# Modulation sums of a two-stage transformer kernel: 512 columns wide, and half of the block pairs summed during the Fourier stage

## What is computed

```python
sc = jax.nn.silu(c)
for l in range(DEPTH):                                  # DEPTH = 2
    mod = (sc @ w_mod[l] + b_mod[l])[:, None, :]        # 1024 -> 6144
    sh1, sc1, g1, sh2, sc2, g2 = jnp.split(mod, N_MOD, axis=-1)
    u = modulate(rms_norm(h, norm1_g[l]), sh1, sc1)
    if l % 2 == 0:    # Fourier mixing and neighbourhood attention, then w_out
        y, yc = even_mixer(u, uc, ...)
    else:
        y = pool_mixer(u, ...)
    h = h + g1 * y
    h = h + g2 * sq_relu_mlp(modulate(rms_norm(h, norm2_g[l]), sh2, sc2), w_mlp1[l], w_mlp2[l])
```

## Time and profile before

| | |
|---|---|
| runs (3) | 2247.85 us median, 2245.47 to 2248.17 |
| profiled execution | span 2244.5 us; its whole time is not listed, the median of the runs is 3.35 above |
| mean granted TensorE clock | 0.960 |
| PE busy | 2097.8 us (93%) |
| DVE busy | 972.6 us (43%) |
| POOL busy | 793.6 us (35%) |
| ACT busy | 684.9 us (31%) |
| DMA | 224.25 MB, mean 100 GB/s |

### The profile page before, as it was taken

How to read it: one execution, slowest core, us unless ns; L and a number is a source line. 1 busy time by engine, 2 the same in 40 slices (tenths; PEclk the granted TensorE clock), 3 DMA queues, 4 the chain that set the end, 5 groups by cost and what they waited for, 6 DMA issues and landing times. The chain is left out here.

```text
span 2244.5 us, 25972 instructions
## 1 busy us (share of the span) xinstructions
PE 2097.8 (93%) x10180; PEld 1690.7 (75%) x10180; DVE 972.6 (43%) x1696; ACT 684.9 (31%) x912; POOL 793.6 (35%) x240
## 2 busy tenths in 40 slices
PE   7998998799999979999998979999996998999998
PEld 3876576587878867888886747888885876888886
DVE  1575469677595735233142281014444123312122
ACT  2322352222122233222123373245543233222122
POOL 2322123344444443444444203442321443444444
PEclk9899999799999979999999999999997999999999
DMA  8163004242352232222222102222120222222221
GB/s 344 44 239 80 1 32 173 115 188 112 150 224 111 100 124 75 94 93 95 106 98 81 57 1 93 94 75 76 57 76 19 97 91 76 94 94 99 105 77 38
DMA packets 42773, 224.25 MB, mean 100 GB/s; under 512 B 12736, under 2 KB 13248, under 8 KB 17216
## 3 DMA queue, kind: packets, MB, share of 16 engines
q1 hardware_dynamic: 42688, 223.08, 27.4%
HBM read 218.86 MB, written 2.10 MB: 98 GB/s over the span
## 5 line engine op out<-in xcount | busy, mean ns | idle before, releaser
L815 POOL TENSOR_TENSOR wl<-raw,wh 128x2048 fp32r<-128x2048 f32 (+1 forms) x155 | 710.9, 4587 | 1279.0 <-ACT wh L461 1279.0
L896 PE MATMUL bank<-uh,wh 128*128 128x512 f32 x1480 | 592.4, 400 | 31.4 <-POOL wl L815 7.3
L897 PE MATMUL bank<-ul,wh 128*128 128x512 f32 x1480 | 583.9, 394 | 0.0
L898 PE MATMUL bank<-uh,wl 128*128 128x512 f32 x1480 | 583.6, 394 | 0.0
L461 ACT ACTIVATE wh<-raw 128x2048 fp32r<-128x2048 f32 (+1 forms) x155 | 292.8, 1889 | 601.6 <-PE bank L898 588.7
L896 PEld LDWEIGHTS bank<-uh,wh 128*128 128x128 f32 x1480 | 283.2, 191 | 98.5 <-issue 27.2
L896 PE MATMUL bank<-ah,wh 128*128 128x512 f32 x816 | 322.8, 396 | 6.4 <-DVE al L1720 6.4
L898 PEld LDWEIGHTS bank<-uh,wl 128*128 128x128 f32 x1480 | 282.5, 191 | 60.7
L897 PEld LDWEIGHTS bank<-ul,wh 128*128 128x128 f32 x1480 | 283.2, 191 | 58.9 <-issue 1.0
L898 PE MATMUL bank<-ah,wl 128*128 128x512 f32 x816 | 320.6, 393 | 0.0
L897 PE MATMUL bank<-al,wh 128*128 128x512 f32 x816 | 317.7, 389 | 0.0
(11 more groups left out here) (211 smaller groups left out, 2100.2 us busy)
## 6 DMA issues: line engine op xcount, KB each, us to landing
raw<-in_w SPq DMA_DIRECT2D x64, 1024.0 KB, 6.7
mraw<-in_w_modr SPq DMA_DIRECT2D x40, 1024.0 KB, 4.9
raw<-in_w_gu SPq DMA_DIRECT2D x22, 1024.0 KB, 4.9
raw<-in_w_hg SPq DMA_DIRECT2D x16, 1024.0 KB, 4.9
modf<-in_w_modf SPq DMA_DIRECT2D x8, 1024.0 KB, 17.8
raw<-in_w_in SPq DMA_DIRECT2D x8, 1024.0 KB, 17.8
raw<-in_w_out SPq DMA_DIRECT2D x8, 1024.0 KB, 6.0
raw<-in_w_dn SPq DMA_DIRECT2D x8, 1024.0 KB, 4.9
```

The lines of the kernel that those rows point to most:

```text
L815: pool.tensor_tensor(wl[:, b % 2, 0:nk], raw[:, b % RAW, 0:nk], f32(wh[:, b % 2, 0:nk]), ALU.subtract).then_inc(split_lo, 1)
L896: pe.matmul(out, ah_, bh, start=first, stop=False)
L897: pe.matmul(out, ah_, bl, start=False, stop=False)
L898: return pe.matmul(out, al_, bh, start=False, stop=last)
```

## The change

- A load keeps its 1 MB but has another shape: 512 columns of half of the 1024 rows, [128, 4, 512] instead of [128, 8, 256]. Loads 2p and 2p + 1 are a pair; `mod_sum(2p)` does chunks 0 to 3 and `mod_sum(2p + 1)` chunks 4 to 7 into the same `acc[p % 2]`, 512 wide. A load is four dependent DVE instructions instead of eight. There are 40 loads and 20 pairs.
- `mod_columns(p)` does four one-column matmuls per pair, `mod_store(p)` stores four columns.
- Pair 0 and pair 1 (loads 0 to 3) stay beside the projections: pair 0 where block 0 stood, pair 1 behind the first half of product 2, where block 1 stood. Nothing of it is beside products 3 to 7.
- Pairs 2 to 5 (loads 4 to 11, `MOD_EARLY` = 4 to `MOD_MID` = 12) are summed during the Fourier stage, each pair's columns behind `fourier_out(g)`. Their buffers `mmid0` and `mmid1` alias the upper halves of `uh` and `ul`; the first load waits for the end of product 7. Their columns go to bank 0.
- Pairs 6 and 7 stay in w_out, behind products 9 and 11. In mlp0 the columns stand behind blocks 1, 3 and 5 of each iteration.
- SP loads cs, w4 and tab earlier, once load 3 is summed, and the mask (moved to another address) later, once the last y is done.
- The constant 1/1024 goes; norms of 1024 use 1/128 and a scale in the root.

Core of the diff:

```diff
+MOD_EARLY, MOD_MID = 4, 12
+        mmid0 = at("mmid0", [P, 4, 2 * BC], F32, 24 * KB)
+        mmid1 = at("mmid1", [P, 4, 2 * BC], F32, 40 * KB)
-        mraw = at("mraw", [P, 2, KC, BC], F32, A + 48 * KB)
+        mraw = at("mraw", [P, 2, 4, 2 * BC], F32, A + 48 * KB)
...
+        def mod_bank(p):
+            return bank[0] if MOD_EARLY <= 2 * p < MOD_MID else bank[7]
+        def mod_part(m):
+            if MOD_EARLY <= m < MOD_MID:
+                return (mmid0, mmid1)[m % 2][:]
+            return mraw[:, m % 2]
...
-                sp.dma_start(mraw[:, m % 2], t["w_modr"][count(m, q, per)]).then_inc(mraw_full[m % 2], 16)
+                if m == MOD_EARLY:
+                    wait_block(sp, 7)
+                sp.dma_start(mod_part(m), t["w_modr"][count(m, q, per)]).then_inc(mraw_full[m % 2], 16)
...
-                load_mod(b)
+                if b < MOD_EARLY:
+                    load_mod(b)
...
+            load(9, t["w_out"][1])
+            for m in range(MOD_EARLY, MOD_MID):
+                load_mod(m)
+            sp.wait_ge(y_full, 2 * FG)
+            sp.dma_start(mask[:], t["mask"]).then_inc(tab_in, 16)
+            for b in range(10, 12):
+                load(b, t["w_out"][b - 8])
             sp.wait_ge(smax, len(ITEMS))
-            for m in range(PROJ, MOD0):
+            for m in range(MOD_MID, MOD0):
                 load_mod(m)
...
+            def mod_columns(p, q=0, per=0):
+                if per or p:
+                    pe.wait_ge(mcol_used, p + per // 2 * q if per else p)
+                mod_summed(pe, 2 * p + 1, q, per)
+                for a in range(4):
+                    last = pe.matmul(mod_bank(p)[:, a:a + 1], acc[:, p % 2, P * a:P * a + P], one_col, start=True, stop=True)
                 last.then_inc(mcol_full, 1)
...
-                    if half == 0:
-                        mod_columns(b - 1)
+                    if half == 0 and b == 2:
+                        mod_columns(1)
...
             for g in range(FG):
                 fourier_y(g)
                 fourier_out(g)
+                if g == 0:
+                    pe.wait_ge(bank_free[bank_of(6, 0)], used(6) + 1)
+                mod_columns(MOD_EARLY // 2 + g)
...
             for b in range(8, 12):
-                product(b, uh, ul, after=lambda half: mod_columns(PROJ + 2 * (b - 8) + half))
+                product(b, uh, ul)
+                if b % 2:
+                    mod_columns(MOD_MID // 2 + (b - 8) // 2)
...
-                        if layer == 0 and j < 6:
-                            mod_columns(MOD0 + j, q, 6)
+                        if layer == 0 and j in (1, 3, 5):
+                            mod_columns(MOD0 // 2 + j // 2, q, 6)
...
+                a, part, k0 = acc[:, m // 2 % 2], mod_part(m), 4 * (m % 2)
+                if m % 2 == 0:
+                    dve.tensor_scalar(a, part[:, 0], csil[:, 0, 0:1], None, ALU.mult).then_inc(macc, 1)
+                for k in range(1 - m % 2, 4):
+                    dve.wait_ge(macc, n + k)
+                    dve.scalar_tensor_tensor(a, part[:, k], csil[:, k0 + k, 0:1], a, ALU.mult, ALU.add).then_inc(macc, 1)
...
+            mod_sum(MOD_EARLY)
+            mod_sum(MOD_EARLY + 1)
             for g in range(FG):
+                if g < FG - 1:
+                    mod_sum(MOD_EARLY + 2 * g + 2)
+                    mod_sum(MOD_EARLY + 2 * g + 3)
                 dve.wait_ge(four_hi, g + 1)
                 dve.tensor_tensor(ul[:, g, :], bank[4 + g % 2][:], f32(uh[:, g, :]), ALU.subtract).then_inc(four_lo, 1)
+                mod_store(MOD_EARLY // 2 + g)
...
-            mod_sum(PROJ)
-            mod_sum(PROJ + 1)
+            mod_sum(MOD_MID)
+            mod_sum(MOD_MID + 1)
             for b in range(8, 12):
                 for half in range(2):
                     add_to_h(b, 2 * (b - 8) + half, mod(0, 2, 2 * (b - 8) + half), 0)
+                if b == 8:
+                    mod_sum(MOD_MID + 2)
+                    mod_sum(MOD_MID + 3)
```

More of the change, by code:

```diff
@@ L124, in build_program @@
         diag = at("diag", [P, 4, P], F32, A + 76 * KB)
-        mask = at("mask", [P, 3, 256], F32, A + 88 * KB)
-        acc = at("acc", [P, 2, BC], F32, A + 88 * KB)
+        mask = at("mask", [P, 3, 256], F32, A + 84 * KB)
+        acc = at("acc", [P, 2, 2 * BC], F32, A + 88 * KB)
         ah = at("ah", [P, KC, S], F32R, A)
@@ L231, in build_program @@
         epsq_col = con[:, C_EPSQ:C_EPSQ + 1]
-        PROJ = 8
         def f32(x):
@@ L385, in _ @@
                     sp.dma_start(dfts[:], t["dfts"]).then_inc(dft_in, 16)
-            for b in range(8, 12):
-                if b == 10:
-                    mod_summed(sp, PROJ - 1)
+                    mod_summed(sp, MOD_EARLY - 1)
                     sp.dma_start(cs[:], t["cs"]).then_inc(w4_in, 16)
@@ L941, in norm_sum @@
                 for a in range(n // P):
-                    pe.matmul(sums_[:, a:a + 1], norm_sqs(name)[:, P * a:P * a + P], ones_d[:, 0:1], start=(a == 0), stop=False, skip_group_check=True)
+                    pe.matmul(sums_[:, a:a + 1], norm_sqs(name)[:, P * a:P * a + P], ones_v[:, 0:1], start=(a == 0), stop=False, skip_group_check=True)
                 pe.wait_ge(sq_ready, 8 * i + 8)
                 for a in range(n // P):
-                    last = pe.matmul(sums_[:, a:a + 1], sq[:, 1, P * a:P * a + P], ones_d[:, 0:1], start=False, stop=(a == n // P - 1), skip_group_check=True)
+                    last = pe.matmul(sums_[:, a:a + 1], sq[:, 1, P * a:P * a + P], ones_v[:, 0:1], start=False, stop=(a == n // P - 1), skip_group_check=True)
                 last.then_inc(sum_full, 1)
                 pe.wait_ge(diag_ready, i + 1)
-                pe.matmul(rms[:, 0:n], ones_d, diag[:, 0:n // P, :].rearrange("p a n -> p (a n)"), start=True, stop=True).then_inc(rms_full, 1)
-            def mod_columns(m, q=0, per=0):
-                if per or m:
-                    pe.wait_ge(mcol_used, count(m, q, per))
-                mod_summed(pe, m, q, per)
-                for a in range(2):
-                    last = pe.matmul(bank[7][:, a:a + 1], acc[:, m % 2, P * a:P * a + P], one_col, start=True, stop=True)
+                pe.matmul(rms[:, 0:n], ones_v, diag[:, 0:n // P, :].rearrange("p a n -> p (a n)"), start=True, stop=True).then_inc(rms_full, 1)
+            def mod_columns(p, q=0, per=0):
[4 more added lines that the diff above has]
+                    last = pe.matmul(mod_bank(p)[:, a:a + 1], acc[:, p % 2, P * a:P * a + P], one_col, start=True, stop=True)
                 last.then_inc(mcol_full, 1)
@@ L1012, in _ @@
                 product(b, uh, ul, after=beside(b))
-            mod_columns(PROJ - 1)
             pe.wait_ge(w4_in, 32)
@@ L1380, in mod_sum, with mod_store @@
             def mod_sum(m, q=0, per=0):
[L1382 removed]
+                n, p = (4 * m + 4 * per * q, m // 2 + per // 2 * q) if per else (4 * m, m // 2)
+                a, part, k0 = acc[:, m // 2 % 2], mod_part(m), 4 * (m % 2)
                 dve.wait_ge(mraw_full[m % 2], 16 * (m // 2 + 1) + 8 * per * q if per else 16 * (m // 2 + 1))
[L1384 to L1387 removed]
+                if m % 2 == 0:
+                    if per and m == MOD0:
+                        dve.wait_ge(mcol_full, p)
+                    elif m >= 4:
+                        dve.wait_ge(mcol_full, p - 1)
+                    dve.tensor_scalar(a, part[:, 0], csil[:, 0, 0:1], None, ALU.mult).then_inc(macc, 1)
+                for k in range(1 - m % 2, 4):
                     dve.wait_ge(macc, n + k)
[L1389 to L1393 removed]
+                    dve.scalar_tensor_tensor(a, part[:, k], csil[:, k0 + k, 0:1], a, ALU.mult, ALU.add).then_inc(macc, 1)
+            def mod_store(p, q=0, per=0):
+                dve.wait_ge(mcol_full, p + 1 + per // 2 * q if per else p + 1)
+                c = 16 + 4 * p
                 if per:
                     c = c + 2 * per * q
[L1396 removed]
+                    out, b = modc[:, bass.ds(c, 4)], bmod[:, bass.ds(c, 4)]
                 else:
[L1398 to L1399 removed]
+                    out, b = modc[:, c:c + 4], bmod[:, c:c + 4]
+                dve.tensor_tensor(out, mod_bank(p)[:, 0:4], b, ALU.add).then_inc(mcol_used, 1)
             dve.wait_ge(const_in, 48)
@@ L1434, in _ @@
             mod_sum(2)
+            mod_sum(3)
+            mod_store(1)
             for b in range(2, 8):
                 for half in (-1, 0, 1):
[L1437 to L1438 removed]
                     if (b, half) in HN_AFTER:
                         hn_scale(HN_AFTER[b, half])
[L1441 to L1443 removed]
             for a in range(2):
```

54 lines of the change are left out of this document (16 added, 38 removed).

## The result

The changed kernel takes 2227.4 us (median of 4 runs, 2222.1 to 2229.0) against 2246.8 of the kernel before beside it (4 runs, 2245.5 to 2248.2): a ratio of **0.9907, 95% interval 0.9894 to 0.9921**. Measured again later, it took 2227.8 (ratio 0.9907, 0.9891 to 0.9924). The forecast was 2225.0, so the sum of -22.9 us met a measured -19.4 (difference of the medians) to -20.9 (by the ratio). One microsecond of the forecast came from its base, 2247.85, the median of three runs; with four it is 2246.8.

The account below looks back on a forecast made before the run. PE was taken as the bound, busy 93% of the span, so time is PE time plus its holes. Terms 21.7 - 15.8 - 0.9 + 3.3 - 13.1 - 3.9 - 14.2 = -22.9 from 2247.85 gave 2225.0 us, range 2216 to 2233.

Parts of the forecast that it names:

- Part 1: Block 2: PE stands 18.3 us before pair 1's columns, waiting for late load 3; head sum 1 comes 21.7 us later.
- Part 2: Projections: without sums 4 to 7 on DVE, no kT or qT waits, -15.8 us; two column groups fewer, -0.9.
- this stays: Claim that DVE stays blocked while POOL splits; a narrow first instruction had taken 4.42 us instead of 0.35.
- Part 3: Fourier: four pairs summed there cost +3.3 us for columns; sums ready 1.5 us ahead at the first pair.
- Part 4: w_out: four sums instead of eight, -13.1 us; then the norm before mlp0, with an earlier load of block 12, -3.9.
- Part 5: mlp0: shorter waits for sums and fewer column groups, 369.0 us, so -14.2; bounds -17 and -10.
- the 0.3 us that stood beside the sum: mlp0: a wide DVE operation could hold a POOL split 0.3 us longer, making the forecast sum 0.3 higher.
- The price of a sum: DVE: a load as four dependent 512-wide instructions of 0.77 us takes 3.0 us; bounds 2.8 and 3.96.
- Rival A: Wide instructions save little, 3.96 us per load; parts 1, 5 and 4 grow by 0.9, 4 and 1: 2231 us; chance 0.10.
- B: Projection holes come back through the norm chain; part 2 gives 3 instead of 15.8: 2237.8 us; chance 0.07.
- C: No wait at block 2, load 3 in time gives 20 us more: 2205 us; chance 0.04.
- D: Slower than before: Fourier-stage loads are slow, 4 loads - 27 us; 2269 us at 17.8 us loads; chance 0.05.

Follow-up runs that it names:

- The third experiment: Changed kernel with load 3 issued ahead of vwin, plus no pair in Fourier: two pairs back beside products 3 to 7, two in w_out; 2210.7 us, ratio 0.9837.
- its narrow twin: Load 3 ahead of vwin, no pair in Fourier, each 512-wide sum instruction split into two of 256 columns; 2247.3 us, ratio 1.0003 to the kernel before.
- the narrow kernel: Changed kernel with every 512-wide sum instruction split into two of 256 columns, same places otherwise; 2234.8 us, ratio 0.9956 to the kernel before.
- the slowed loads: Changed kernel with two extra unused 1 MB loads ahead of each of the eight Fourier-stage loads; 2252.6 us, ratio 1.0023 to the kernel before.
- the kernel without it: Changed kernel with load 3 issued on SP ahead of the 32 vwin transfers; 2205.4 us, ratio 0.9812 to the kernel before.
- the kernel with the columns later: Changed kernel, SP's order kept, pair 1's columns and store one block later, behind product 3's first half; 2205.2 us, ratio 0.9814 to the kernel before.
- the square of four kernels: All with load 3 ahead of vwin; no pair in Fourier: narrow 2247.3, wide 2210.7 us; four pairs there: narrow 2214.9, wide 2205.1 us.

## Why the prediction held, point by point

**Part 1, +21.7.** Right in mechanism and size: a wait of 17.0 us against 18.3, since the load came 1 us earlier than before (126.4 against 127.3), and head sum 1 at +21.5. That the last figure is so close is two small errors against each other: from the columns to head sum 0 passed 15.6 us, where the terms of the prediction give 14.9. The experiments show that this wait, its shadow at the low clock included, is 20 to 21 us.

**Part 2, -15.8 and -0.9.** Right in size: 51.0 us from head sum 1 to head sum 9 against 50.7, Fourier at 212.45 against 211.9. The reason was incomplete. I took the sums' presence on DVE for the cause, and expected from moving them what the width alone would have brought as well. The third experiment, which puts two pairs back and finds no hole, and its narrow twin, which finds three, show that the width closes them too; by the rows the holes hang on whether POOL's split meets a sum. I had read the blocked rows but held that "this stays".

**Part 3, +3.3.** Right: four groups of 0.95, each starting the next work 0.8 us later, +3.5 over the stage, and a cover of 1.4 us at the first pair. That the cover is so small is shown by the narrow kernel, whose first pair takes 1.9 us longer to sum and has a wait of 0.68, and by the slowed loads.

**Part 4, -13.1 and -3.9.** Right: 44.55 us to the last columns, and from there 8.8 us to mlp0; -17.75 in all. 

**Part 5, -14.2.** Slightly too much: 370.46 us against 369.0. The first iteration's wait was 1.17 (1.5 allowed), the others' 0.3 to 0.4 (0.6 allowed), so the error isn't in the waits for acc. The groups of columns take 1.05 us behind a wait and 0.95 otherwise, 11.8 in all instead of 11.2. The term that was left at nothing is the clock behind the wait that remains. I had taken it out together with the nine microseconds, but from 1.3 us behind the first columns a stretch of 3.4 us runs at 1.2 GHz:

```profile
427.20:430.60 3.40, 3.40 (x10) 2.63 (x9) 3.40 (x2) 0.01 (x1) 3.31 (x1) 0.50 0.89 347
```

That is 1.7 us lost by estimate (half of 3.4), and 354.5 + 11.8 + 2.3 of waits + 1.7 are 370.3. POOL's busy time here is 159.1 us as before, so the wide operations don't hold the splits longer in sum, and the 0.3 us that stood beside the sum didn't show; single splits are held in both kernels, up to 5.17 us instead of 4.6 after the change and up to 5.11 before.

**The price of a sum.** 3.0 us taken; 3.11 measured, and 2.85 for a load that begins with the cheaper first instruction. It was right for an undisturbed sum. Rival A's price of the width (+6) came near the 7 us measured for this kernel, but by luck: mlp0's share was over 9 us against the 4 I gave it, attention added 3, and untouched code gave 7 back in the profiled executions. As a statement about width it was far too small: at the places of before it is 36.6 us.

**Rivals.** A: a wide load costs 2.8 to 3.1, not 3.96. B: the norm chain holds up nothing but 0.41 us. C: the wait was there; its price, "2205", is what the kernel without it took. D: above.

**Where the last 3 to 5 us went.** Untouched stages. Attention was 2.4 us shorter, mostly by its first 22 us running at a clock of 0.85 instead of 0.77. From mlp1's first product on the kernel took 5.3 us longer, and the granted clock shows where. The stretch of 50 us that starts about 850 us behind that product (columns as in the earlier trace rows), before first, then after, then the kernel with the columns later, which behind that product takes 7 us less than the changed kernel:

```profile
1694.77:1744.77 50.00, 33.41 (x160) 27.54 (x161) 25.18 (x37) 19.54 (x26) 4.63 (x1) 0.73 0.03 8
```

```profile
1671.37:1721.37 50.00, 33.97 (x157) 27.84 (x156) 23.87 (x35) 18.30 (x25) 1.41 (x1) 0.66 0.04 17
```

```profile
1649.10:1699.10 50.00, 33.03 (x173) 26.82 (x170) 26.14 (x39) 20.00 (x26) 4.62 (x1) 0.80 0.05 17
```

The same code runs more of its time at 1.2 GHz in one execution than in another: 0.73, 0.66 and 0.80. These rows alone don't make it a property of the kernel, since the runs of one kernel differ as much: the changed kernel took 2222.1 us at a mean clock of 0.965 and 2229.0 at 0.960, the one with the columns later 2199.3 at 0.969 (the profiled execution) and 2208.0 at 0.964. Both profiles of the changed kernel are of its slower executions (2228.2 and 2228.9). So the 5.3 us lie within what the executions of one kernel differ by, and the profiles can't say whether the change has a part in them. What sets the share of the low clock stays open.

## What to carry to other kernels

Before a reader is moved or merged with another, look up when its latest input is issued on its queue: here two equal inputs merged into one pair made PE wait 17 us for a load that stood behind 20 us of small transfers, and one moved line gave it back. Where two engines block each other, look at each place whether the meeting goes. Beside the projections 1 us less per sum took all four sums out of the way of a 4.6 us split and brought 18 us, many times its length. In mlp0 the shorter sums met more splits than the long ones, and the 10 to 12 us there came from less work on DVE. And two changes that close the same hole don't add up; the square of four kernels shows it, where single steps from one end would have credited either with nearly all.

## What the runs showed of the hardware that I had not expected

- A sum of two SBUF inputs on DVE stands for as long as a split on POOL, up to 5.18 us for one instruction of 0.75, and so does the TENSOR_SCALAR that begins it, 4.42 us for one of 0.35, while the reciprocal beside a split kept its 3.35 us in every row of the projections.
- The clock behind a wait isn't set by the wait's length alone: eight column matmuls take 1.84 us instead of 0.95 behind the 17 us wait, 1.45 and 1.56 behind two of 2.0 and 2.2 us, and behind a wait of 3.2 us for acc in mlp0's first iteration 1.05 in one narrow kernel and 1.87 in another. The 2 us that the prediction takes for each long hole can't hold for every one of them.
- Identical code is granted different shares of the low clock from one execution to the next, worth 7 to 10 us of 2200 among the runs of one kernel (2222.1 to 2229.0, 2199.3 to 2208.0, 2196.7 to 2206.8), with mean clocks from 0.960 to 0.970 to match. It bounds how closely a sum of terms can be compared with a time, whatever the terms.
